# A two-layer decoder trunk: the layer loop written out in full, and no memory prepared behind the last layer

## What is computed

```
for l in range(2):
    h = rms_norm(x, g0);  z = h @ w_in[l]
    mix = [dilated attention (6 heads), spatial gating, retention (6 heads)](z)
    x = x + rms_norm(mix @ w_out[l], g1)
    mem_n = rms_norm(mem, g6)                    # 256 memory tokens
    x = x + rms_norm(memory_attention(rms_norm(x, g2), mem_n, x_wq, x_wkv, x_wo), g3)
    f = square(relu(rms_norm(x, g4) @ w_up[l])) @ w_down[l]
    x = x + rms_norm(f, g5)
```

## Time and profile before

| | us |
|---|---|
| median of 3 runs | 1597.31 (1596.2 to 1598.82) |
| the profiled execution: its own time | 1596.7 |
| the profiled execution: its span | 1594.9 |
| PE busy, of the span | 1558.5 |
| DVE busy | 697.9 |
| ACT busy | 575.7 |
| POOL busy | 174.2 |

### The profile page before, as it was taken

One profiled execution on the slowest core, in us unless ns is written; L12 is line 12 of the kernel. 1 busy time (PEld: TensorE's weight loads), 2 busy tenths in 40 slices (PEclk: granted clock), 3 DMA queues, 4 the chain that ended last, 5 costly groups with the idle time before them and its releaser, 6 DMA issues.

```text
span 1594.9 us, 21583 instructions
## 1 busy us (share of the span) xinstructions
PE 1558.5 (98%) x8008; PEld 1326.1 (83%) x8008; DVE 697.9 (44%) x840; ACT 575.7 (36%) x870; POOL 174.2 (11%) x195
## 2 busy tenths in 40 slices
PE   5999999999999999999999999999999999999997
PEld 5978798888888888888888788988888888888886
DVE  5323256624464342433571233656245434434345
ACT  5335334434343231313352443335344322322232
POOL 2001520300120000000030017102001100000001
PEclk9999999999999999999999999999999999999999
DMA  7332122341123323233333122125202233233332
GB/s 242 113 93 86 60 80 80 122 143 54 54 80 106 100 84 106 80 136 114 108 126 113 60 87 86 61 80 179 85 27 80 83 103 97 92 102 105 120 118 80
DMA packets 79966, 156.40 MB, mean 98 GB/s; under 512 B 3584, under 2 KB 19712, under 8 KB 79872
## 3 DMA queue, kind: packets, MB, share of 16 engines
q1 hardware_dynamic: 78000, 149.98, 28.3%
q10 hardware_dynamic: 1440, 3.56, 0.6%
q0 software_dynamic: 432, 1.57, 0.3%
HBM read 153.01 MB, written 2.10 MB: 97 GB/s over the span
## 4 chain that ended last, share of the span: by engine, by line
PE 90%; DVE 3%; issue 3%; ACT 2%; DMA 1%; POOL 1%; DVEq 0%; ACTq 0%; POOLq 0%; SPq 0%
PE proj L547 27%; PE proj L549 26%; PE proj L548 26%; PE work L596 2%; PE work L576 2%; PE work L612 1%; PE work L604 1%; ACT w_hi L906 1%; PE work L730 1%; PE work L709 1%; PE work L684 1%; DVE w_lo L1150 1%; DMA w_raw<-in_x_wkv_dram 1%; ACT x_probs L993 0%; DVE x_top L1332 0%
## 5 line engine op out<-in xcount | busy, mean ns | idle before, releaser
L1150 DVE TENSOR_TENSOR w_lo<-w_raw,w_hi 128x2048 fp32r<-128x2048 f32 (+1 forms) x137 | 301.1, 2198 | 483.1 <-ACT w_hi L906 480.4
L906 ACT ACTIVATE w_hi<-w_raw 128x2048 fp32r<-128x2048 f32 (+1 forms) x137 | 250.1, 1825 | 480.7 <-PE proj L549 474.3
L547 PE MATMUL proj<-hT_hi,w_hi 128*128 128x512 f32 (+1 forms) x800 | 299.2, 374 | 4.6 <-DVE w_lo L1150 4.6
L549 PE MATMUL proj<-hT_hi,w_lo 128*128 128x512 f32 (+1 forms) x800 | 298.1, 373 | 0.0
L548 PE MATMUL proj<-hT_lo,w_hi 128*128 128x512 f32 (+1 forms) x800 | 298.1, 373 | 0.0
L547 PE MATMUL proj<-w_hi,hT_hi 128*128 128x512 f32 (+1 forms) x640 | 240.6, 376 | 1.2 <-DVE hT_lo L1211 1.2
L549 PE MATMUL proj<-w_hi,hT_lo 128*128 128x512 f32 (+1 forms) x640 | 232.4, 363 | 0.0
L548 PE MATMUL proj<-w_lo,hT_hi 128*128 128x512 f32 (+1 forms) x640 | 231.9, 362 | 0.0
L547 PE MATMUL proj<-w_hi,uT_hi 128*128 128x512 f32 x512 | 199.6, 390 | 0.0
L549 PE MATMUL proj<-w_hi,uT_lo 128*128 128x512 f32 x512 | 199.2, 389 | 0.0
L548 PE MATMUL proj<-w_lo,uT_hi 128*128 128x512 f32 x512 | 199.2, 389 | 0.0
(11 more groups left out here) (156 smaller groups left out, 1684.6 us busy)
## 6 DMA issues: line engine op xcount, KB each, us to landing
w_raw<-in_w_up_dram SPq DMA_DIRECT2D x32, 1024.0 KB, 5.5
w_raw<-in_w_down_dram SPq DMA_DIRECT2D x32, 1024.0 KB, 5.0
w_raw<-in_w_in_dram SPq DMA_DIRECT2D x28, 768.0 KB, 4.4
w_raw<-in_x_wkv_dram SPq DMA_DIRECT2D x17, 1024.0 KB, 5.2
w_raw<-in_w_out_dram SPq DMA_DIRECT2D x8, 1024.0 KB, 5.7
w_raw<-in_x_wq_dram SPq DMA_DIRECT2D x8, 1024.0 KB, 5.2
w_raw<-in_x_wo_dram SPq DMA_DIRECT2D x8, 1024.0 KB, 5.0
gains<-in_norm_g_dram SPq DMA_DIRECT2D x13, 512.0 KB, 6.2
```

The lines of the kernel that those rows point to most:

```text
L547: nc.tensor.matmul(dst, l_hi, r_hi, start=first, stop=False)
L549: return nc.tensor.matmul(dst, l_lo, r_hi, start=False, stop=last)
L906: nc.scalar.activation(w_hi[:, slot, :, 0:cols], w_raw[:, slot, :, 0:cols], ACT.Copy).then_inc(w_hi_done, 1)
L1150: nc.vector.tensor_tensor(w_lo[:, slot, :, 0:cols], w_raw[:, slot, :, 0:cols], w_hi[:, slot, :, 0:cols].bitcast(F32), ALU.subtract).then_i ...
```

## The change

The layer loop is written out: `for l in range(DEPTH)` in Python in place of the hardware loop, on all five engines, so every wait with no group register in it compares with a constant. The inner loops over MLP groups stay hardware loops. `sem_inc(waits_passed, 1)` goes everywhere but in SP's group loop (the diff has some 35 such lines; a few stand here). In the last layer everything that prepares memory or a block for a further layer is left out.

```diff
         def values(eng, *counts):
-            return [eng.snap(count) for count in counts]
+            return [count if isinstance(count, int) else eng.snap(count) for count in counts]
...
                     sp.wait_ge(w_lo_done, nth(w_lo_done, l, b - WSLOTS + 1))
-                    sp.sem_inc(waits_passed, 1)
...
-            with sp.Fori(0, DEPTH) as l:
+            for l in range(DEPTH):
...
-                load_block(l, BLOCKS, x_wkv[DEPTH - 1:DEPTH, 0:BK * P, 0:512])
+                if l < DEPTH - 1:
+                    load_block(l, BLOCKS, x_wkv[l + 1:l + 2, 0:BK * P, 0:512])
...
-                            if last and name == "dn0" and kb == 1 and t < MT:
+                            if last and l < DEPTH - 1 and name == "dn0" and kb == 1 and t < MT:
                                 turn_normed(l, "memk", t)
...
-            with pe.Fori(0, DEPTH) as l:
+            for l in range(DEPTH):
...
             def mlp_group(l, g, last):            # ACT; DVE has the same with split_lo
                 for i in range(GROUP_BLOCKS):
                     b = HEAD_BLOCKS + i
-                    if i > 0:
+                    if i > 0 and not (last and l == DEPTH - 1 and i == GROUP_BLOCKS - 1):
                         split_hi(l, b + 1, g=g)
-                    if last and i == 0:
+                    if last and l < DEPTH - 1 and i == 0:
                         act.wait_ge(turned, nth(turned, l, 2 * TURNED["n3", T - 1] + 2))
...
-                    if last and i == 5:
+                    if last and l < DEPTH - 1 and i == 5:
                         for t in range(MT):
                             turn_hi(l, ("memk", t), memT_hi, t)
...
-                    if last and i == 4:
+                    if last and l < DEPTH - 1 and i == 4:
                         for t in range(MT):
                             norm_mem(l, "memk", t)
-                    if last and i == 5:
+                    if last and l < DEPTH - 1 and i == 5:
                         for t in range(MT):
                             turn_lo(l, ("memk", t), memT_hi, memT_lo, t)
...
                 pool.wait_ge(summed, nth(summed, l, r + 1))
-                pool.sem_inc(waits_passed, 1)
                 nc.gpsimd.tensor_tensor(meansq[:, r % 2], sumsq[:, r % 2], half_mean[:, t:t + 1], ALU.add).then_inc(pool_link, 1)
                 pool.wait_ge(pool_link, nth(pool_link, l, next(links)))
-                pool.sem_inc(waits_passed, 1)
```

More of the change, by code:

```diff
@@ L582, in turned_in @@
                 pe.wait_ge(turned_lo, nth(turned_lo, l, 2 * TURNED[key] + 2))
-                pe.sem_inc(waits_passed, 1)
             def a_scores(l, u):
@@ L1054, in mlp_group @@
                         act.dma_start(gains[:, GAIN_SLOT["mem"]],
-                                      norm_g[DEPTH - 1:DEPTH, GAIN["mem"]].broadcast_to([P, D])).then_inc(gain_loaded["mem"], 16)
-                    if last and i == 5:
+                                      norm_g[l + 1:l + 2, GAIN["mem"]].broadcast_to([P, D])).then_inc(gain_loaded["mem"], 16)
+                    if last and l < DEPTH - 1 and i == 5:
                         for t in range(MT):
@@ L1084, in _ @@
                 act.dma_start(dst[:], src).then_inc(const_loaded, 16)
-            with act.Fori(0, DEPTH) as l:
+            for l in range(DEPTH):
                 for b in range(HEAD_BLOCKS):
@@ L1220, in a_step @@
                     dve.wait_ge(p_turned, at1)
-                    dve.sem_inc(waits_passed, 1)
                     nc.vector.tensor_tensor_reduce(out=probs[:, j % 2, 0:n], in0=work[:, j % 2, 0:n],
@@ L1449, in _ @@
                 turn_lo(PROLOGUE, ("memk", t), memT_hi, memT_lo, t)
-            with dve.Fori(0, DEPTH) as l:
+            for l in range(DEPTH):
                 links = itertools.count(1)
@@ L1545, in _ @@
                 pool.dma_start(xs[:, t], x[0, t * P:(t + 1) * P]).then_inc(x_loaded[t], 16)
-            with pool.Fori(0, DEPTH) as l:
+            for l in range(DEPTH):
                 links = itertools.count(1)
```

4 lines of the change are left out of this document (removed).

## The result

The changed kernel takes 1585.51 us (median of four runs, 1584.65 to 1587.88), the kernel before 1596.76 beside it on the same chip (1596.14 to 1598.82). The ratio is 0.993, with a 95% interval of 0.9916 to 0.9944.

What follows compares the result with a forecast made beforehand. PE was taken as the bound, busy 1558.5 of 1594.9 us. Savings 1.7 + 2.05 + 2.05 = 5.8, plus 1.5 for the clock, took 1596.7 to 1589.4, or 1590.0 us on the median's scale; range 1586.8 to 1593.8.

Steps and rivals of the forecast that it cites:

- Part 1: Last layer's preparations go: PE sees only the 16 transposes in two calls, 1.7 us saved (ends 1.6 and 1.8).
- Part 2: Between the layers: the hardware loop's return goes, PE starts block 1 2.05 us earlier (ends nothing and 2.1).
- DVE is what is late next: Between the layers: DVE's `w_lo`, behind its last update, then sets PE's start of block 1, leaving a 1.2 us stall.
- Part 3: Waits on constants without counting, on all paths to PE: 2.05 us saved (ends 0 and 3.6).
- PE's other short waits in mixer and cross attention, and the first loads: Remaining short PE waits, and first loads that SP issues behind register work: 0.3 us saved (ends 0 and 1).
- Register instructions on PE itself cost nothing: On PE, without any waits: register instructions cost nothing, read from 10.00 of 10.00 us busy at an MLP group loop's return.
- Part 4: The granted clock, which falls after PE's stalls: one fall fewer than the two before, 1.5 us saved.
- less often when shorter: Clock falls follow shorter PE stalls less often; the stalls ahead of the MLPs were to shrink from 2.3 to 1.9 us.
- those about the clock: Rivals on the clock's falls: two as before, 1591.5 us (chance 0.25); or none at all, 1588.5 us (0.2).
- only work counts: Rival: links are hidden or cost the same with constants, Part 3 gives nothing, clock stays; 1593.6 us (chance 0.07).
- the idle time is not the return: Rival: at the layer's head the 2.05 us stay without the jump; 1593.6 us, or 1595.6 (chance 0.06 together).
- slower: Rival: written-out layer 1 code is slow to fetch, four stalls of 3.7 us, 14.8 against 7.3 gained; 1604.8 us (chance 0.02).

Runs made afterwards that it cites:

- e1: The changed kernel with the last layer's preparations for a further layer kept; 1587.36 us.
- e7: e1 with the layer loop put back as a hardware loop on DVE alone, with DVE's counts; 1594.03 us.
- e3: e1 with the layer loop put back as a hardware loop on PE alone; 1588.23 us.
- e13: The kernel of e3 run and profiled once more, unchanged; 1590.11 us in one run.
- e9: The kernel before with the layers written out on PE alone, all counts and the other engines' loops kept; 1595.74 us.
- e4: e1 with the layer loop put back as a hardware loop on ACT alone; 1587.77 us.
- e5: The changed kernel with the counting increments put back on DVE alone; 1588.62 us.
- e11: The changed kernel with the counting increments put back on PE and SP alone; 1585.88 us in one run.
- e6: The changed kernel with the counting increments put back on POOL alone; 1587.94 us.
- e16: The kernel before, unchanged, profiled a third time; 1598.56 us in one run.
- e15: The kernel of e9 run and profiled once more, unchanged; 1596.87 us in one run.
- e2: The changed kernel with all counting increments put back on SP, PE, DVE and POOL, layers still written out; 1591.42 us.
- e12: The changed kernel, unedited, profiled once more; 1587.62 us in one run.
- e14: The kernel of e11 run and profiled once more, unchanged; 1587.47 us in one run.
- e8: The kernel before, unedited, profiled a second time; 1599.39 us in one run.

## Why the prediction was wrong in size and right in kind

**Part 1 was right.** 1.7 us forecast. The stretch says 1.9 in e1, for both calls of transposes and what lies about them. The tail was put at nothing and has some 0.10 of it.

**Part 2 was right, at its size nearly too.** 2.05 forecast, 1.9 measured. The step "DVE is what is late next" holds: e7 alone brings the whole loss back, e3, e13 and e9 show PE's return to be worth nothing there, and e4 ACT's 0.45. The stall left over was put at 1.2 us and is 1.65. The last update did not come 0.3 us earlier. From the end of the update before it to its own start it is 1.04 us before the change and after (804.75 to 805.79; 801.38 to 802.42). POOL's rows in between, before the change and after it:

```profile
803.69 1.10 POOL L1515 TENSOR_TENSOR meansq<-sumsq,half_mean 128x1 f32<-128x1 f32 x1 [0.76 <-ACT squares L926]
804.97 0.78 POOL L1518 TENSOR_TENSOR rstd<-meansq,minus_half 128x1 f32<-128x1 f32 x1 [0.18 <-POOL meansq L1515]
```

```profile
800.22 1.20 POOL L1492 TENSOR_TENSOR meansq<-sumsq,half_mean 128x1 f32<-128x1 f32 x1 [0.76 <-ACT squares L917]
801.51 0.88 POOL L1494 TENSOR_TENSOR rstd<-meansq,minus_half 128x1 f32<-128x1 f32 x1
```

`meansq` ends 0.04 us behind DVE's update both times (804.79; 801.42), and `rstd` takes 0.88 us behind the shorter link where it took 0.78, so the 0.10 of the link is not gained.

The idle times of three engines in the earlier trace rows were rightly read as one thing, and the sizes of two of them were no measure of its price.

**Part 3 is the failed step**, in its term "PE's other short waits in mixer and cross attention, and the first loads", put at 0.3 us with ends of 0 and 1. It measured 3.5: 1.1 us a layer at places that the forecast had not named, and 1.3 at the start. All of Part 3 came to 5.2 us (bodies 3.9, start 1.3), where 2.05, with an upper end of 3.6, were forecast. Term by term:
- A link on POOL is 0.10 us dearer with a count, not 0.14; on DVE 0.10, as taken. Ahead of the MLP the way from the first root to the update was 450.86 - 449.01 = 1.85 us and is 447.52 - 445.88 = 1.64 (the earlier trace rows and the rows of after above): 0.21 a layer instead of 0.42.
- The wait behind the group norm went whole, 0.62 a layer and not 0.3. DVE's three links are 0.3 of it, as forecast: with DVE's counts alone (e5) a wait of 0.29 is back. Another 0.2 is the count behind PE's own wait, which the prediction left out (0.20 in e11). The last 0.1 is not settled. 0.62 was the bound that the prediction named.
- The remaining 1.1 us a layer (1.92 - 0.62 - 0.21) are many places of 0.1 to 0.3 us, most of which the timeline does not even show as a wait of PE. One is in cross attention of layer 0. Timelines of PE and of DVE, before the change, then the same two after it:

```profile
392.78 1.95 PE L730 MATMUL work<-x_probsT,vm 128*128 128x128 f32 x16
394.86 0.65 PE L717 MATMUL work<-ident,x_probs 128*128 128x128 f32 x4
```

```profile
393.81 0.16 DVE L1325 RECIPROCAL x_rden<-x_den 128x2 f32<-128x2 f32 x1
394.12 0.69 DVE L1329 TENSOR_TENSOR x_probs<-x_probs,x_rden 128x512 f32<-128x512 f32 x1
```

```profile
390.02 1.95 PE L723 MATMUL work<-x_probsT,vm 128*128 128x128 f32 x16
391.80 0.60 PE L710 MATMUL work<-ident,x_probs 128*128 128x128 f32 x4
```

```profile
390.47 0.16 DVE L1309 RECIPROCAL x_rden<-x_den 128x2 f32<-128x2 f32 x1
390.67 0.69 DVE L1312 TENSOR_TENSOR x_probs<-x_probs,x_rden 128x512 f32<-128x512 f32 x1
```

PE's step from the one group to the next was 394.86 - 392.78 = 2.08 us, and ended 0.05 after DVE's `x_probs` (394.12 + 0.69 = 394.81). It is 391.80 - 390.02 = 1.78 now, with `x_probs` ready at 391.36. The link itself is 0.11 shorter (0.20 for 0.31); that the rest comes from the links before it is likely, not shown. So the chains of counted links on DVE and POOL were in places a little longer than PE's work beside them, and a sum over the waits that the list shows does not see that. e5, e6 and e11 give the shares: 2.2 us DVE, 1.1 POOL, 0.5 PE and SP.
- At the end of the span 0.3 was forecast and nothing came: without a fall before has 355.64 there (e16), and e1's kernel with one engine looping 355.68 to 355.72 (e3, e7, e13). POOL's counts alone add nothing either (353.71 in e6), for the reason shown at Part 2.
- The first loads: 1.3 us, and not by SP's register work, which e9 and e15 have and start at 28.07 and 28.47 with, but with PE's loop.

"Register instructions on PE itself cost nothing" was nearly right: e3 against e1 has them at 0.18 us a layer. The stretch read for it in the earlier trace rows is one in which PE waits for nothing.

**Part 4 was right in that falls get fewer; how many is chance.** The boundary's stall of 1.65 us had no fall in eight profiles (after, e1, e2, e5, e6, e11, e12, e14); before's, 2.08 to 2.25 us, had one in all three, and e7's, e9's and e15's of 3.5 as well, e4's of 2.10 none. That is the one fall fewer of the forecast. For the MLP's stalls the step "less often when shorter" has less behind it: they shrank from 2.28 to 2.17 us, not to 1.9. Over all profiles 10 of 22 such stalls of 2.07 to 2.21 us were followed by a fall, and 11 of 14 of 2.27 to 2.42. The changed kernel had none behind these stalls in one profile and two in the other. The 1584.65, 1584.8, 1586.21 and 1587.88 us of its four runs stand some 1.5 apart; falls of none, none, one and two would give that, but only the first was profiled.

**The sum.** Bodies 3.9, boundary 1.9, end 1.9 and start 1.3 make 9.0 us, where 5.8 were forecast. Of the 11.25 us between the medians some 2.2 are left for the clock, between one fall and two, where 1.5 were forecast. By the rivals: those about the clock each happened in some execution; "only work counts" falls with e2 and "the idle time is not the return" with e7; against "slower", layer 1 runs its new code in 422.92 us where layer 0 took 422.96.

By the rule of the Trainium skill that the prediction drew on ("Runtime: NRT & Kernel Launch", section "Instruction fetch mechanics") the long return is a fetch; the traces agree as far as they go: 0.7 us of idle time on PE in e3, 2.07 on ACT in e4, 1.76 on DVE in e7, and none of PE at the short loops that stay (after the change it is busy in 330.0 of the 330.0 us from 460 to 790). The fetch itself is in none of them.

**Still open:** how PE's code comes to delay a load that ACT issues. A kernel with PE's loop but its code placed otherwise was not tried. What an engine does in the idle time of its loop's return isn't shown either, only that it goes when the loop is written out. Nor is it settled why the same stall of 2.17 us is followed by a fall in one execution and not in the next.

## What to carry to other kernels

Where several engines lose time at one place, the price is that of the engine whose work is late for the bottleneck: put the loop back for one engine at a time before the others are looked at. A cost that is small but stands in each link of a chain beside a busy engine must be counted over the whole chain and compared with the slack of that chain, and not over the waits that the list of waits names. With medians that move by single steps of the clock, the time between two fixed points of two traces tells apart 0.1 us, if no fall lies between them, where the medians can't tell 1.5.

## What the runs showed of the hardware that was not expected

- A count behind a wait costs 0.10 us on DVE and on POOL, in the link that follows it (0.14 against 0.04; 0.18 against 0.08), and 0.20 on PE behind its wait for `hT_lo` (e11). It comes to 3.8 us over the two layers (e2), where no single wait of PE grows by more than 0.6.
- The return of the layer loop costs each engine time of its own. ACT stands idle 2.07 us with its loop alone and 1.99 to 2.36 with the others', DVE 1.76 alone and 1.76 to 1.83 with the others', PE 0.66 to 0.69 alone (e3, e13) but 1.06 to 1.22 with all five (before, e8, e16).
- A stall of 2.17 us is followed by the lower clock level in one execution (e12) and not in another of the same program; a fall costs 1.41 to 1.66 us.
- A first load of 64 KB takes 3.2 to 3.5 us to land in all five profiles with a hardware loop around PE's layers, and in eleven of the thirteen without 1.8 to 2.7; the other two have 2.9 and 3.3.
